# Gate and up projections of a feed-forward stage by Strassen's seven block products in place of eight

## What is computed

```python
h = rms_norm(x, g_ffn)
x = x + (jax.nn.silu(h @ w_gate) * (h @ w_up)) @ w_down
```

## Time and profile before

| | us |
|---|---|
| median of three executions | 3720.39 |
| the profiled execution, its own time | 3726.19 |
| its span, first to last instruction | 3724.6 |
| TensorE busy in the span | 3379.1 |
| VectorE busy | 1407.2 |
| ACT busy | 1015.3 |
| feed-forward matmuls, first start to end | 2169.3 to 3695.0 |

### The profile page before, as it was taken

How to read it: one execution, slowest core, us unless ns; L and a number is a source line. 1 busy time by engine, 2 the same in 40 slices (tenths; PEclk the granted TensorE clock), 3 DMA queues, 4 the chain that set the end, 5 groups by cost and what they waited for, 6 DMA issues and landing times. The chain is left out here.

```text
span 3724.6 us, 67944 instructions
## 1 busy us (share of the span) xinstructions
PE 3379.1 (91%) x29423; PEld 3102.5 (83%) x29423; DVE 1407.2 (38%) x1761; ACT 1015.3 (27%) x1402; POOL 578.7 (16%) x697
## 2 busy tenths in 40 slices
PE   6999996769859999678779989999999999999997
PEld 6999996458837777454439989999999999999997
DVE  3222221833345665146633243333333333333334
ACT  4111111623215665134402132222122122122112
POOL 2000000534514333362000000000000000000000
PEclk8999998679979999769989999999999999999999
DMA  7433333455525442464143233233333233333332
GB/s 212 114 114 112 109 87 109 152 159 143 142 85 228 180 191 91 140 177 94 37 170 100 70 91 91 91 91 91 91 91 91 91 91 91 93 94 95 94 92 92
DMA packets 490816, 426.40 MB, mean 114 GB/s; under 512 B 124725, under 2 KB 439590, under 8 KB 485918
## 3 DMA queue, kind: packets, MB, share of 16 engines
q1 hardware_dynamic: 468222, 300.40, 28.8%
q0 software_dynamic: 20736, 122.13, 9.3%
q10 hardware_dynamic: 1600, 0.01, 0.0%
HBM read 382.99 MB, written 66.78 MB: 121 GB/s over the span
## 5 line engine op out<-in xcount | busy, mean ns | idle before, releaser
L2779 DVE TENSOR_TENSOR f_w_lo<-wo_raw,f_w_hi 128x2048 fp32r<-128x2048 f32 x132 | 302.5, 2292 | 813.1 <-ACT f_w_hi L2751 813.1
L53 PE MATMUL d_ps<-hh,f_w_hi 128*128 128x260 f32 x2816 | 567.6, 283 | 11.3 <-DVE f_w_lo L2779 11.3
L57 PE MATMUL d_ps<-hh,f_w_lo 128*128 128x260 f32 x2816 | 568.2, 283 | 0.0
L55 PE MATMUL d_ps<-hl,f_w_hi 128*128 128x260 f32 x2816 | 567.3, 283 | 0.0
L2751 ACT CAST f_w_hi<-wo_raw 128x2048 fp32r<-128x2048 f32 x132 | 252.1, 1910 | 998.1 <-DMA wo_raw<-in_w_gate 400.7
L53 PEld LDWEIGHTS d_ps<-hh,f_w_hi 128*128 128x128 f32 x2816 | 435.1, 189 | 11.9 <-DVE f_w_lo L2779 11.8
L57 PEld LDWEIGHTS d_ps<-hh,f_w_lo 128*128 128x128 f32 x2816 | 434.9, 189 | 0.0
L55 PEld LDWEIGHTS d_ps<-hl,f_w_hi 128*128 128x128 f32 x2816 | 433.6, 189 | 0.0
L53 PE MATMUL p_ps<-xh,p_w_hi 128*128 128x264 f32 (+2 forms) x1504 | 306.8, 285 | 10.8 <-DVE p_w_lo L306 10.8
L2702 POOL TENSOR_TENSOR mix_raw<-mix_raw 128x520 f32<-128x520 f32 x44 | 57.4, 1306 | 1621.7 <-ACT mix_raw L2760 1621.7
L55 PE MATMUL p_ps<-xl,p_w_hi 128*128 128x264 f32 (+2 forms) x1504 | 306.3, 285 | 0.0
(11 more groups left out here) (456 smaller groups left out, 5054.2 us busy)
## 6 DMA issues: line engine op xcount, KB each, us to landing
p_w<-in_w_in SPq DMA_DIRECT2D x46, 1024.0 KB, 5.6
wo_raw<-in_w_gate SPq DMA_DIRECT2D x44, 1024.0 KB, 5.6
wo_raw<-in_w_up SPq DMA_DIRECT2D x44, 1024.0 KB, 5.6
wo_raw<-in_w_down SPq DMA_DIRECT2D x44, 1024.0 KB, 5.1
wo_raw<-in_w_o SPq DMA_DIRECT2D x16, 1024.0 KB, 6.0
rk_chunks<-r_outb POOLq DMA_DIRECT2D x8, 1280.0 KB, 6.2
s_cur<-rk_chunks SPq DMA_DIRECT2D x8, 1280.0 KB, 7.2
s_one_vecs<-samp_rows SPq DMA_DIRECT2D x80, 128.0 KB, 4.7
```

The costliest lines, as they stand in the source:

```text
L53: pe.matmul(out[j], w_hi, x_hi[j], start=start, stop=False)
L55: pe.matmul(out[j], w_hi, x_lo[j], start=False, stop=False)
L57: last = pe.matmul(out[j], w_lo, x_hi[j], start=False, stop=stop)
L2779: dve.tensor_tensor(w_lo[:, s, :], w_raw[:, s, :], w_hi[:, s, :].bitcast(F32), ALU.subtract).then_inc(lo_done, 1)
```

## The change

The stage now has 22 parts of two tiles of hidden columns, and 18 units of 512 KB (1024 elements per partition) in a part. For gate and for up, the product of D x 2 tiles of weights with the activations is taken as 2 x 2 blocks (half of D, one tile, one half of the rows) and made of seven products (A11, S2, S3, S1, A12, S4, A22, in this order), each of 8 blocks x 3 matmuls. Four of the weight operands are sums: S1 = A21 + A22, S2 = S1 - A11, S3 = A11 - A21, S4 = A12 - S2, made by VectorE in the block's own slot or in one of three extra slots. The low part overwrites the raw weights. The seven matching operands of the activations, normalised first, are made and split once at the stage's start and stay in SBUF. The four quarters of each result are put together by VectorE and ACT from the four banks (`quarters`), and the hidden quarters are split by both. Then four down units of 48 matmuls follow, each in two halves `d` of four banks. POOL takes part only in the start. There are six slots for raw weights: A11 of gate and of up and the first down unit share slot 0; both A21 and the second down unit share slot 1; the other two down units go to the slots of up's A12 and A22. In `stage_out_proj`, POOL now clears the semaphores of the attention stages before it loads; buffers of that stage are given back ahead of the new stage.

```diff
--- before.py
+++ after.py
             def _(pool):
+                clear_old(pool, g)
                 for q in range(4, 8):
                     pool.wait_ge(mix_lo, q - 3)
                     mix_load(pool, g, q)
...
     HC = TC // 2
-    HT = 4
-    PARTS = D_FF // P // HT
...
-    GR = 12
...
+    KH = KT // 2
+    PARTS = D_FF // P // 2
...
+        A11, S2, S3, S1, A12, S4, A22 = range(PC)
+        LOADS = (3, 3, 1, 1, 2, 2)
+
+        def slot_of(n):
+
+            if n >= 2 * PC:
+                return (0, 1, 4, 5)[n - 2 * PC]
+            q, m = n // PC, n % PC
+            return {A11: 0, S3: 1, A12: 2 + 2 * q, A22: 3 + 2 * q}.get(m)
...
+        def weights(n, loads=raw, added_up=sums):
+            q, m = n // PC, n % PC
+            s = slot_of(n)
+            t = loads[:, s] if s is not None else added_up[:, {S1: 0, S2: 1, S4: 2}[m]]
+            return t.rearrange("p (k n) -> p k n", k=KH if q < 2 else 2)
...
+                def load(i, n, done=None):
+                    s, q, m = slot_of(n % W), n // PC, n % PC
+                    if n == W + A11:
+                        src = gate_v[:, 0:KH, 2 * P:][:, :, bass.ds(i * (2 * P), P)]
+                        n = A11
+                    elif q < 2:
+                        p, c = {A11: (0, 0), A12: (1, 0), S3: (0, 1), A22: (1, 1)}[m]
...
+                        src = (gate_v, up_v)[q][:, p * KH:(p + 1) * KH, bass.ds(at, P)]
                     else:
...
+                        at = i * 2 if isinstance(i, int) else sp.snap(i * 2, min_val=0, max_val=D_FF // P - 2)
+                        src = down_v[:, bass.ds(at, 2), m * 512:(m + 1) * 512]
+                    if done is not None:
+                        sp.wait_ge(used, done)
+                    sp.dma_start(weights_f(n), src).then_inc(loaded[s], 16)
...
-                    for n in range(UN - 3 if last else UN):
-                        sp.wait_ge(summed, i * SUMS + through(n))
-                        load(i, n + 3)
+                    for done, n in ((1, PC + A11), (3, PC + S3), (5, W + A12), (7, W + A22), (8, 2 * PC), (10, 2 * PC + 1),
+                                    (12, 2 * PC + 2), (14, 2 * PC + 3), (15, W + A11), (16, W + S3),
+                                    (17, W + PC + A12), (18, W + PC + A22)):
+                        if not (last and n >= W):
+                            load(*(later(i, n) if n != W + A11 else (i, n)), i * W + done)
                 with nc.allow_non_contiguous_dma(reason="one value to a partition"):
...
-                for n in range(3):
+                for n in (A11, S3, A22, A12, PC + A12, PC + A22):
                     load(0, n)
...
+                pool.wait_ge(scaled, 4)
+                pool.tensor_tensor(t_f[:, A12], t_f[:, A12], rstd[:, 0].unsqueeze(1).to_broadcast([P, KH, HC]),
+                                   ALU.mult).then_inc(pool_normed, 1)
+                pool.wait_ge(normed, 3)
+                pool.tensor_tensor(t_f[:, S3], t_f[:, S4], hid_f[:].rearrange("p v a h t -> p (v a h) t"),
+                                   ALU.subtract).then_inc(t3_made, 1)
...
-                def part(i, first):
-                    for n in range(2 * HT):
-                        j, m, s = n // 2, n % 2, n % 3
-                        pe.wait_ge(lo_done, i * UN + n + 1)
-                        if m == 0:
-
-                            pe.wait_ge(freed, i * GR + j + 1)
-                        for k in range(KT):
-                            if first and n == 0:
-                                pe.wait_ge(h_lo, k + 1)
-                            cols = slice(k * P, (k + 1) * P)
-                            last = three_products(pe, [bank(j, 2 * m + h) for h in range(2)], w_hi[:, s, cols], w_lo[:, s, cols],
-                                                  halves(g.hh, k), halves(g.hl, k), k == 0, k == KT - 1)
-                        last.then_inc(summed, 1)
...
-                            last.then_inc(summed, 1)
+                def pair(i, q):
+                    at = 4 * q
+                    banks = {A11: at, A12: at, S2: at + 1, S3: at + 2, A22: at + 2, S1: at + 3, S4: at + 3}
+                    for m in range(PC):
+                        n = q * PC + m
+                        pe.wait_ge(lo_done, i * W + n + 1)
+                        if i == 0 and q == 0:
...
+                        if m == A12:
+                            pe.wait_ge(p1_kept, i * 2 + q + 1)
+                        if m == S4:
+                            pe.wait_ge(u4_made, i * 2 + q + 1)
+                        if m == A22:
+                            pe.wait_ge(c22_made, i * 2 + q + 1)
+                        out = ps[:, banks[m], 0:HC]
+                        for k in range(KH):
...
+                            pe.matmul(out, w, xh, start=(m < 4 and k == 0), stop=False, skip_group_check=True)
+                            pe.matmul(out, w, xl, start=False, stop=False, skip_group_check=True)
+                            last = pe.matmul(out, wl, xh, start=False, stop=(k == KH - 1), skip_group_check=True)
+                        last.then_inc(used, 1)
...
+                def down(i, c):
+                    n = 2 * PC + c
+                    pe.wait_ge(lo_done, i * W + n + 1)
+                    for e in range(2):
+                        d = 2 * c + e
+                        at = 4 * e
+                        if c:
+                            pe.wait_ge(freed, i * GR + d - 1)
+                        else:
+                            pe.wait_ge(c21_made, i * 2 + e + 1)
+                            pe.wait_ge(gate_freed, i + 1)
+                        for k, h in ((0, 0), (0, 1), (1, 1), (1, 0)):
+                            if d == 0 and h == k:
+                                pe.wait_ge(hid_ready, i * 3 + 2)
+                            if d == 0 and k > h:
+                                pe.wait_ge(hid_ready, i * 3 + 3)
+                            for m in range(2):
...
+                        last.then_inc(used if e else half_done, 1)
+
                 for i in range(PARTS):
-                    part(i, i == 0)
+                    for q in range(2):
+                        pair(i, q)
+                    for c in range(DN):
+                        down(i, c)
...
                 def high(i, n):
-                    s = n % 3
-                    act.wait_ge(loaded[s], i * (16 * UN // 3) + (n // 3 + 1) * 16)
-                    act.copy(w_hi[:, s, :], w_raw[:, s, :]).then_inc(hi_done, 1)
+                    if slot_of(n) is None or n % PC == S3 and n < 2 * PC:
+                        q, m = n // PC, n % PC
+                        act.wait_ge(added, (i * 2 + q) * 4 + {S1: 1, S2: 2, S3: 3, S4: 4}[m])
+                    else:
+                        wait_loaded(act, i, n)
+                    if not isinstance(i, int) or i * W + n >= 3:
+                        act.wait_ge(used, i * W + n - 2)
+                    act.copy(high_of(n), weights_f(n)).then_inc(hi_done, 1)
...
+                    for n in range(W):
+                        q, m = n // PC, n % PC
+                        if q and m < 2:
+                            quarters(i, q - 1, m + PC)
+                        if not last or n + 2 < W:
+                            high(*later(i, n + 2))
+                        if q < 2:
+                            quarters(i, q, m)
...
+                act.wait_ge(var_ready, 1)
+                act.activation(rstd[:], rstd[:], ACT.Sqrt).then_inc(root_ready, 1)
                 act.wait_ge(gain_in, 16)
-                for k in range(KT):
...
+                for n, (m, p, j) in enumerate(((A11, 0, 0), (None, 0, 1), (S4, 1, 1), (A12, 1, 0))):
+                    for k in range(KH):
+                        dst = hid_f[:].rearrange("p v a h t -> p (v a h) t")[:, k] if m is None else t_f[:, m, k]
+                        last = act.activation(dst, g.xt[:, p * KH + k, j * HC:(j + 1) * HC], ACT.Copy,
+                                              scale=gain[:, p * KH + k:p * KH + k + 1])
+                    last.then_inc(scaled, 1)
+                    if n == 1:
                         high(0, 0)
-                act.wait_ge(freed, 2)
...
+                for m in range(PC):
...
+                    act.copy(t_hi[:, m], t_f[:, m]).then_inc(th_done, 1)
+                    if m == 0:
+                        high(0, 1)
+                part(0, False)
...
+                def add(i, q, m):
...
+                    count = (i * 2 + q) * 4
+                    a11, a12, a21, a22 = (weights_f(q * PC + n) for n in (A11, A12, S3, A22))
+                    x, y, op, needs = {
+                        S1: (a21, a22, ALU.add, None),
+                        S2: (weights_f(q * PC + S1), a11, ALU.subtract, count + 1),
+                        S3: (a11, a21, ALU.subtract, None),
+                        S4: (a12, weights_f(q * PC + S2), ALU.subtract, count + 2)}[m]
+                    for n in {S1: (S3, A22), S2: (A11,), S4: (A12,)}.get(m, ()):
```

(101 more changed lines are left out.)

244 lines of the change are left out of this document (139 added, 105 removed).

## The result

The changed kernel takes **3810.9 us**, the median of four executions (3809.03 to 3814.24), beside 3718.9 us for the kernel before (four executions, 3712.27 to 3722.6). The ratio is **1.025, 95% interval 1.0233 to 1.0268**: slower. The direction and the range (3703 to 3815) held, but the loss is 92 us where the forecast had 40.

A forecast was written before the change was run, and what follows sets the result against it. TensorE's count of matmuls was taken as the bound; -126.9 + 29.4 + 15.4 + 90.3 + 31.5 = +39.7 us gave 3765.9 us for the profiled execution, 3760.1 against the median, range 3703 to 3815.

The forecast's parts named there:

- 1056 matmuls fewer: Gate and up projections over 22 parts: 7 x 24 matmuls each instead of 8 x 24, at 120.2 ns, -126.9 us.
- one bank: slower pace: Each product's 24 matmuls in one bank instead of two alternating: taken as nothing, bound 5 ns each, 35 us.
- the start, to the third product's end: Stage start: seven input blocks prepared before the products, 72 matmuls done at 2209.4 instead of 2180.0 us, +29.4 us.
- the hidden split: Down projection waits for the hidden block's low parts, 0.7 us in each of 22 parts, +15.4 us.
- the turn of the part: TensorE's fourth down unit waits for VectorE's residual addition behind A21's load and sums: 4.3 us, 21 parts, +90.3 us.
- the clock behind it: Lower TensorE clock after each turn's wait: 1.5 us in each of 21 parts, +31.5 us; bounds nothing and 3.0.
- The landing that no row had: Time for A21's 512 KB weight load to land at the turn: taken as 3.8 us, between 2.8 and 5.6.
- the rival of an early load: A21's load lands soon, 2.2 us, wait 2.7; with the clock held, sum -25.4, 3695 us; chance 0.11.
- the one of a slow load: A21's load takes 5.6 us like the large one: wait 6.1, +37.8 more, 3798 us; chance 0.13.
- The other bound, 3.0: Upper bound on clock loss per turn, from 6.8 us at the lower level behind 3.95 us idle.
- The rival that the clock holds: No lower clock behind the turns' waits: sum +8.2 us, 3729 us; chance 0.14.
- POOL's two multiplies of 2080 elements: Stage start: 4 x 1306 ns each on POOL, claimed to fit beside VectorE's work, no cost added.

The follow-up runs named there:

- e1: Changed kernel with VectorE's residual addition that frees the four banks put ahead of the three weight sums at each turn; 3703.1 us, 0.994 of before.
- e3: Changed kernel with the second down unit in another raw-weight buffer, and the bank-freeing addition put between VectorE's second and third weight sums; 3655.7 us, 0.9824 of before.
- e4: Changed kernel with 30 added matmuls of 252 columns, whose results nothing reads, ahead of the wait at each of 21 turns; 3750.9 us, 1.008 of before.
- e6: Changed kernel with the hidden block's low parts and ACT's last copy put ahead of the second down unit's splits; 3776.0 us, 1.0152 of before.
- e2: Changed kernel with the second down unit in another raw-weight buffer, so A21's load can be issued earlier, VectorE's order unchanged; 3685.9 us, 0.9902 of before.
- e7: Changed kernel with buffer exchange, interleaved turn, hidden low parts first, start's input splits one product ahead, GpSimd's two operations on VectorE; 3624.9 us, 0.9749 of before.
- e5: Changed kernel with GpSimd's two operations of 2080 elements at the stage's start done by VectorE; 3799.2 us, 1.022 of before.

## Why the prediction was right or wrong

Its sum against the profiled executions, which differ by 82.8 us; the measured column is worked out from the steps above and adds, but for rounding, to 82.4, the difference of the last matmuls' starts:

| step of the sum | forecast | measured |
|---|---|---|
| 1056 matmuls fewer | -126.9 | -126.7 |
| one bank: slower pace | 0 (bound 35) | +5.6 |
| the start, to the third product's end | +29.4 | +37.8 |
| the hidden split | +15.4 | +14.5 |
| the turn of the part | +90.3 | +97.9 |
| the clock behind it | +31.5 | +53.4 |

*Matmuls.* Right. Each runs at 0.1205 us where it was 0.1200, so the bank or whatever else sets that half nanosecond lies near the value taken, at 5.6 us.

*The hidden split and the turn.* Right in place and chain, and near in size. The landing that no row had was taken as 3.8 us between 2.8 and 5.6, and the page has 3.8; this spoke against the rival of an early load and the one of a slow load alike. The estimate of 3.2 from the Trainium skill's DMA: Bandwidth & Descriptors (Anatomy of one DMA) was short; the fit there is of transfers that GpSimd issues, and SP issues these. The turn took 4.66 us on the mean of the 21 (4.5 to 5.3), not 4.3. From the first sum to TensorE's restart it is 6.05 us in 20 of the 21, where the forecast had 6.1, so the difference lies ahead of that sum, in the issue and the landing. e1 to e3 take the chain apart: either end of it, the load or the order, leaves 1.7 us, both leave nothing.

*The clock.* **The step that failed**, and the largest error: "so I take 1.5" per turn. Two rows stood for it, 3.4 and 6.8 us at the lower level behind 2.56 and 3.95 us of idleness. I chose the first because TensorE's work behind it was dense. Dense work behind the wait did not shorten it: this is the window behind the turn shown above, and its kind follows 20 of 21 turns:

```profile
2627.90:2634.80 6.90, 5.62 (x26) 5.66 (x27) 4.60 (x5) 0.00 (x0) 0.00 (x0) 0.51 0.02 5
```

The price is 53.4 / 21 = 2.5 us a turn. That is the loss of 6.8 us at the lower level less the part of it that passes while TensorE still waits, and e4 measured it apart, as 2.4. The other bound, 3.0, would have been the better choice. That a wait of 4.66 us lies nearer to the longer row is no proof that its length decides: e6 has both kinds behind waits of the same length, so what picks between them stays open. The rival that the clock holds is refuted for this wait; it holds for the 1.7 us waits of e1 and e2. The rule cited from the Trainium skill's TensorE: Matmul & The Clock Gate (Loop structure matters more than you think), that long waits between matmuls leave the array cold, at the lower clock, agrees with the trace here: the clock of the long window is 0.95, and e7's, with no long waits, 1.00.

*The start.* "POOL's two multiplies of 2080 elements" that "fit beside that" were the second failing step, 8 us (one of the two is a subtraction). I asked only whether POOL ends in time for ACT, not what its work does to VectorE. e5 showed the hold, 4.4 us in one of VectorE's rows and 4.3 in another. The Trainium skill's SBUF — State Buffer, section SBUF: two separate sides, says that VectorE and GpSimd lock a shared pair of ports for a whole instruction, VectorE for operations with two inputs in SBUF too, and that the other one blocks. The trace agrees: VectorE's two rows end 1.1 and 2.2 us behind GpSimd's, where alone they take 1.22 and 2.33.

*The rest.* 92 against 82.8 is the two profiles' place among their own executions, not a step.

*The range.* It holds the measured time partly by luck. Its upper end stood for a slow load with part of the dearer clock, and the load was not slow. The clock (21.9 us over its term), the start (8.4), the turn (7.6), the pace (5.6) and the 9.2 us of the executions brought the time there.

## What to carry to other kernels

This trade of matmuls for work on other engines was paid at the places where those engines' orders join TensorE's, not in their total: a twelfth fewer of the stage's matmuls, with VectorE busy for two thirds of the stage and ACT for one, still lost 92 us, and the same arithmetic with a few lines reordered, one buffer exchanged and GpSimd's two operations on VectorE gained 95. For each wait that a change adds, price the chain from the buffer that comes free to the work that TensorE needs, and put that work ahead of whatever is for later. Then price the clock behind the wait, and where rows of two prices stand for it, don't take the cheaper one because the work around the wait is dense: here the dearer kind followed 20 of 21 turns.

## What was not expected of the hardware

- A VectorE operation with two inputs in SBUF was held for as long as GpSimd's ran: 5.60 us against 1.22, and 6.60 against 2.33.
- The price of a wait jumped between the two lengths seen: 21 waits of some 1.7 us left the clock at its upper level (e2), 21 of 4.7 us cost 2.5 us each beyond themselves. Between, in e1, a wait of 2.67 us from start to start had no fall behind it and those of 2.20 and 2.59 had one of 3.4 us each.
- Taking away a 0.85 us wait in the middle of a part also took 13.5 us of lower clock from the turns, although the waits there stayed as long (e6).
